# Reordered fillings, copies and weight splits in the attention stage of a one-core decoder trunk, with each round's next scores ahead of its values on TensorE

## The reference

```python
DILATED_BRANCHES = ((128, 1), (512, 4), (2048, 16))      # window, dilation

def dilated_branch(q, k, v, window, dilation):           # per head, blocks and their predecessors
    s = jnp.einsum('bhrnqd,bhrnkd->bhrnqk', qb, kk) * (Dh ** -0.5)
    s = jnp.where(mask, s, NEG)
    m = jnp.max(s, axis=-1)
    p = jnp.exp(s - m[..., None])
    l = jnp.sum(p, axis=-1)
    o = jnp.einsum('bhrnqk,bhrnkd->bhrnqd', p, vv) / l[..., None]

def dilated_attention(q, k, v):                          # the branches joined by their own maxima and sums
    wts = ls * jnp.exp(ms - jnp.max(ms, axis=0))
    return einsum(wts, os_) / sum(wts)

def mixer_ab(h, ...):
    z = h @ w_in          # queries, keys, values of both kinds of heads, and a rank-16 gate input
    ...
    return concatenate([oa, ob]) @ w_out
```

## Time and profile before

| | |
|---|---|
| median of 3 runs | 2091.09 us (2089.84 to 2091.24) |
| the profiled execution | 2089.45 us, of which the span of its instructions is 2087.6 us |
| PE busy | 2062.1 us (99%) |
| PEld, DVE, ACT, POOL busy | 81%, 70%, 44%, 42% |
| granted TensorE clock, mean | 0.998 |
| attention's steps in the trace | 223.5 us (first scores) to some 445 us |

### The profile page before, as it was taken

One profiled execution on the slowest core, in us unless ns is written; L12 is line 12 of the kernel. 1 busy time (PEld: TensorE's weight loads), 2 busy tenths in 40 slices (PEclk: granted clock), 3 DMA queues, 4 the chain that ended last, 5 costly groups with the idle time before them and its releaser, 6 DMA issues.

```text
span 2087.6 us, 26260 instructions
## 1 busy us (share of the span) xinstructions
PE 2062.1 (99%) x10166; PEld 1699.6 (81%) x10166; DVE 1467.3 (70%) x1728; ACT 916.9 (44%) x1274; POOL 873.3 (42%) x455
## 2 busy tenths in 40 slices
PE   8999999999999999999999999999999999999997
PEld 6888788878888888888888888888888888888886
DVE  6669775655976676677989504538877667677988
ACT  4231566744544444444435330225544444444444
POOL 3332112232787777760002332444877776820000
PEclk9999999999999999999999999999999999999999
DMA  4111001032222221228983111113321221249872
GB/s 169 41 31 41 21 31 32 31 122 91 81 91 91 91 81 71 91 72 306 389 298 114 51 51 31 51 41 121 111 89 63 91 91 68 84 140 384 302 282 81
DMA packets 95165, 235.95 MB, mean 113 GB/s; under 512 B 10113, under 2 KB 12482, under 8 KB 95042
## 3 DMA queue, kind: packets, MB, share of 16 engines
q1 hardware_dynamic: 93170, 229.54, 30.8%
q10 hardware_dynamic: 1872, 4.74, 0.6%
HBM read 198.59 MB, written 35.65 MB: 112 GB/s over the span
## 4 chain that ended last, share of the span: by engine, by line
PE 93%; DVE 3%; DMA 1%; SPq 1%; issue 1%; ACT 1%; POOL 0%; DVEq 0%; ACTq 0%
PE ps L1419 13%; PE ps L1420 13%; PE ps L1421 13%; PE ps L926 6%; PE ps L929 6%; PE ps L932 6%; PE ps L1453 6%; PE ps L1455 6%; PE ps L1456 6%; PE ps L1133 2%; PE ps L1135 2%; PE ps L1134 2%; PE ps L1524 1%; PE ps L1525 1%; PE ps L1526 1%; PE ps L1282 1%
## 5 line engine op out<-in xcount | busy, mean ns | idle before, releaser
L630 POOL TENSOR_TENSOR w_hi<-w_raw,ones 128x1024 fp32r<-128x1024 f32 x53 | 105.2, 1986 | 694.3 <-PE ps L932 230.2
L1419 PE MATMUL ps<-t_hi,w_hi 128*128 128x512 f32 x672 | 263.7, 392 | 0.3
L1420 PE MATMUL ps<-t_lo,w_hi 128*128 128x512 f32 x672 | 261.8, 390 | 0.0
L1421 PE MATMUL ps<-t_hi,w_lo 128*128 128x512 f32 x672 | 261.6, 389 | 0.0
L1453 PE MATMUL ps<-d_hi 128*128 128x512 f32 (+1 forms) x632 | 242.4, 384 | 0.2 <-DVE d_lo L2226 0.2
L1456 PE MATMUL ps<-d_hi,d_lo 128*128 128x512 f32 (+1 forms) x632 | 241.6, 382 | 0.0
L1455 PE MATMUL ps<-d_lo,d_hi 128*128 128x512 f32 (+1 forms) x632 | 241.6, 382 | 0.0
L690 POOL TENSOR_TENSOR w_lo<-w_sum,w_hi 128x1024 fp32r<-128x1024 f32 x84 | 231.9, 2771 | 23.2 <-ACT w_hi L2758 23.2
L690 POOL TENSOR_TENSOR w_lo<-w_raw,w_hi 128x1024 fp32r<-128x1024 f32 x84 | 157.5, 1875 | 171.0 <-ACT w_hi L2758 157.2
L1419 PE MATMUL ps<-act_hi,w_hi 128*128 128x512 f32 x504 | 196.1, 389 | 0.0
L1420 PE MATMUL ps<-act_lo,w_hi 128*128 128x512 f32 x504 | 196.1, 389 | 0.0
(11 more groups left out here) (348 smaller groups left out, 4540.4 us busy)
## 6 DMA issues: line engine op xcount, KB each, us to landing
w_raw<-w_up SPq DMA_DIRECT2D x44, 1024.0 KB, 4.8
d_ring<-w_dn SPq DMA_DIRECT2D x146, 256.0 KB, 7.9
d_ring<-g_kept SPq DMA_DIRECT2D x124, 256.0 KB, 9.6
g_kept<-gst SPq DMA_DIRECT2D x44, 512.0 KB, 2.6
w_raw<-w_in SPq DMA_DIRECT2D x24, 512.0 KB, 3.5
chain_a<-g_kept SPq DMA_DIRECT2D x44, 256.0 KB, 9.3
x_kept<-x SPq DMA_DIRECT2D x16, 512.0 KB, 9.2
x<-x_kept SPq DMA_DIRECT2D x16, 512.0 KB, 10.2
```

The costliest lines, as they stand in the source:

```text
L1419: pe.matmul(out, wh, bh, start=(fresh and j == 0), stop=False, skip_group_check=True)
L1420: pe.matmul(out, wh, bl, start=False, stop=False, skip_group_check=True)
L1421: ins = pe.matmul(out, wl, bh, start=False, stop=(j == 3), skip_group_check=True)
```

## The change

1. `low_rank` of the first four tiles of x goes behind the third tile of `first_key` (k = 2) and no longer behind the first.
2. In pair 0, GpSimd no longer waits for the end of the rope stages before it splits N_A + 4, and VectorE no longer waits for that split. VectorE's order of `out_step` and `take_part` in steps 0 to 4 changes.
3. `fills_of` leaves two pieces behind the second transposes and no longer one (but not in a pair's last round), and takes the first group from what is left.
4. `v_transposes` go ahead of the step's transposes (steps 0 to 5), in pair 0 a step later, and ScalarE's copies of them ahead of `take`.
5. In each round TensorE does the next round's scores ahead of this round's values.
6. ScalarE does `take_outs` behind the exponentials and no longer ahead.
7. In the last pair step 24 fills first and then does scores 25; `spread` goes behind `take`, in steps 1 to 3. The high part of N_WO + 3 waits for the scores of pair 2, and only the low part for `values(27)`.

```diff
@@ GpSimd @@
             low_part((N_A + 3) % 2, (N_A + 3) % 2, N_A + 5)
-            pool.wait_ge(A.rope, 20)
             low_part((N_A + 4) % 2, (N_A + 4) % 2, N_A + 6)
...
             plain(N_WO + 2, 2, (A.vn, 5 * (NHP - 1) + 3), (WO.lo, 2))
-            plain(N_WO + 3, 3, (A.pv, STEPS_A - 4))
+            n = N_WO + 3
+            pool.wait_ge(s_wdma[n % 2], 16 * (n // 2 + 1))
+            pool.wait_ge(A.s, 2 * DOUBLE)
+            pool.tensor_tensor(w_hi[:, 3, :], w_raw[:, n % 2, :], ones[:, 0:1].to_broadcast([P, 1024]), ALU.mult
+                               ).then_inc(s_whi, 1)
+            pool.wait_ge(A.pv, STEPS_A - 4)
+            low_part(n % 2, 3, n + 2)
@@ lists @@
             both = fill_of(g) + fill_of(g + 1)
-            last = len(both) - (g % SA < SA - 2)
+            last = len(both) - 2 * (g % SA < SA - 2)
             first = last - len(both) // 4
...
-            return {3: ((0, 2),), 4: ((0, 3),)}.get(s, ())
+            return {4: ((0, 2),), 5: ((0, 3),)}.get(s, ())
@@ TensorE @@
-                if k == 0 or k == 4:
+                if k == 2 or k == 4:
                     low_rank(k // 4)
...
                 for i in range(2):
                     for target, j in fills[i]:
                         piece(target, j)
+                    moves = v_moves_of(g + i)
+                    if s < SA - 2:
+                        for target, m in moves:
+                            v_transposes(target, m)
+                        moves = ()
                     transposes(g + i, 0)
                     transposes(g + i, 1)
-                    moves = v_moves_of(g + i)
...
                 for target, j in fills[2]:
                     piece(target, j)
-                for i in range(2):
-                    values(g + i)
                 scores(g + 2)
                 if g + 2 < DOUBLE:
                     scores(g + 3)
+                for i in range(2):
+                    values(g + i)
             for g in range(DOUBLE, STEPS_A):
                 hp, s = divmod(g, SA)
+                if g == DOUBLE:
+                    fill(g)
                 if g + 1 < STEPS_A:
                     scores(g + 1)
-                fill(g)
+                if g > DOUBLE:
+                    fill(g)
@@ VectorE @@
                     if s == 0:
                         take_part(0, Q1, (1, 2))
-                        dve.wait_ge(s_wsplit, N_A + 5)
-                        out_step(1, 0, 0)
-                        out_step(1, 0, 1)
+                        for step_n in range(2):
+                            out_step(1, 0, step_n)
...
                     elif s == 2:
                         take_part(1, K0, (1, 2))
-                        for step_n in range(2):
+                        take_part(1, Q0, (0,))
+                        out_step(1, 1, 0)
+                    elif s == 3:
+                        for step_n in range(1, 3):
                             out_step(1, 1, step_n)
-                    elif s == 3:
-                        take_part(1, Q0, (0,))
-                        for step_n in range(2, 5):
+                        dve.wait_ge(B.o[1], 8)
+                        take_part(1, Q0, (1, 2))
+                    elif s == 4:
+                        for step_n in range(3, 5):
                             out_step(1, 1, step_n)
-                    elif s == 4:
-                        take_part(1, Q0, (1, 2))
@@ ScalarE @@
                 if g:
-                    take_outs(g - 2)
                     if s == 0:
                         statistics_exp(hp - 1)
                     exps(g)
                     exps(g + 1)
+                    take_outs(g - 2)
                 if hp and s in (2, 4):
                     spread(hp - 1, s - 1)
+                moves_taken(g)
                 take(g, 0)
                 take(g, 1)
-                moves_taken(g)
...
+                if s == 4:
+                    moves_taken(g + 1)
                 take(g + 1, 0)
                 take(g + 1, 1)
-                moves_taken(g + 1)
+                if s != 4:
+                    moves_taken(g + 1)
...
             for g in range(DOUBLE, STEPS_A):
                 hp, s = divmod(g, SA)
                 if s == 0:
-                    take_outs(g - 2)
                     statistics_exp(hp - 1)
                     exps(g)
-                if 1 <= s < 5:
-                    spread(hp - 1, s - 1)
+                    take_outs(g - 2)
+                if s == 1:
+                    spread(hp - 1, 0)
...
                 if hp == NHP - 1:
+                    if 1 <= s < 4:
+                        spread(hp - 1, s)
                     for kk in WO_HIGHS[s]:
```

More of the change, by code:

```diff
@@ L478, in build @@
         STEPS_A = SA * NHP
+        DOUBLE = SA * (NHP - 1)
         R_A = 6 * NBP
@@ L835, in score_stat @@
             return a_class[:, hp % 2, s - NEAR, i:i + 1]
-        DOUBLE = SA * (NHP - 1)
         def scores_bank(g, h):
```

## The result

| | before | after |
|---|---|---|
| median of 10 runs each | 2091.3 us (2089.5 to 2093.5) | 2096.8 us (2095.0 to 2100.5) |
| profiled execution, and its span | 2089.45, 2087.6 us | 2098.7, 2096.9 us |
| PE busy | 2062.1 us | 2068.0 us |
| mean granted TensorE clock | 0.998 | 0.995 |

The ratio of after to before is 1.0026 (95%: 1.0018 to 1.0035): 5.5 us slower. The predicted time, 2094.7 us, is 2.1 us low. The result lies in the range and in the forecast's own one, but just over the bound of 0.2%, so that "slower" holds, to which I had given 0.29, and not "within 0.2%", to which I had given 0.55. The interval reaches down to 0.18%, so it is a narrow call. The two profiled executions lie further apart than the medians, 9.3 us: before's is near the fast end of its kernel's times, and after's the second slowest of its ten.

A forecast was written before the change was run, and what follows sets the result against it. TensorE, busy 99% of the span, bounds the kernel. Terms −0.2 + 0.3 − 1.0 + 1.7 + 2.8 = +3.6 us take the median from 2091.09 to 2094.7 us; the 8 in 10 range is 2085.0 to 2098.5.

The forecast's parts named there:

- the forecast's own one: The main forecast's own range, 2092.5 to 2097 us, with a chance of 0.48.
- the bound of 0.2%: What a measurement of this kernel can tell from no change: about 0.2%, 4.2 us.
- start: Moved product of four x tiles: the third tile ends 0.2 us sooner, −0.2; bounds −1.7 and +1.7.
- pair 0: Two stalls of 1.2 and 1.6 us merge into two others; V0 starts about when it did: +0.3.
- rounds of pairs 1 and 2, with g = 22: Both waits for a_vc go, −1.0; `take_outs` ahead of `take` costs 0.4 us at g = 22.
- turn to the last pair: Scores 25's wait goes, −1.6, but TensorE idles 2.7 us for V0: +1.7 with g = 22's 0.4.
- end of the steps, from g = 25: GpSimd's high and low part each fall ahead of one `attention_low`; TensorE ends the steps 2.8 us later: +2.8.
- behind the attention: TensorE's work after the attention: nothing moves, as no stall that VectorE or GpSimd sets is within reach.
- Sharing by bandwidth: VectorE and GpSimd share the SBUF port pair by bandwidth: collisions cost 2.5 not 4.3 us, the end about +1.
- the stalls go and nothing takes their place: Rival, chance 0.16: the attention's seven stalls are covered, V0 taken within 1.6 us of scores 25: 2084.1 us.
- the end doesn't collide: Rival, chance 0.17: at the end of the steps +2.8 becomes about 0, the sum +0.8: 2091.9 us.
- `take` stalls 12 times: Rival, chance 0.14: `take_outs` ahead of `take` stalls second transposes in most of 12 rounds, 3.6 us more: 2098.3 us.

The follow-up runs named there:

- e2_split_back: Changed kernel, but the high part of N_WO + 3 waits for values(27) again, as before: 2092.7 us, ratio 1.0011.
- e3_start_back: Changed kernel, but low_rank of the first four x tiles is behind the first tile of first_key again: 2095.5 us, ratio 1.0024.
- e9_pause_long: Kernel before with four added TensorE pauses of 3.0 to 3.1 us idle in the projections for pairs 2 and 3: 2110.3 us, ratio 1.0090.
- e11_split_only: Kernel before with only the high part of N_WO + 3 put behind the last paired exponentials, its low part still behind values(27): 2091.6 us, ratio 1.0007.
- e6_best: Changed kernel with V0 ahead of tops(25), N_WO + 3's split and the start as before, and another new pair 0 order: 2084.6 us, ratio 0.9966.
- e1_v0_first: Changed kernel, but at the turn to the last pair VectorE takes V0 ahead of tops(25): 2093.2 us, ratio 1.0009.
- e7_swap_only: Kernel before with edit 5 alone, the next round's scores ahead of this round's values: 2089.2 us, ratio 0.9990.
- e8_pause_short: Kernel before with four added TensorE pauses of 1.2 us idle in the projections for pairs 2 and 3: 2095.3 us, ratio 1.0024.
- the last kernel: e6_best, but the split of N_WO + 3 waits for the output projection's first results instead of values(27): 2083.3 us, ratio 0.9967.

## Why the prediction was right in its places and low in its size

Each term against the shift of after's profile, with the stretches at half clock apart. One of 3.41 us is put at 1.6, as above. For the turn, `e2_split_back` and `e3_start_back` have V0's wait of 2.9 us without a stretch and lose 1.8 us each from g = 23 to g = 25; after loses 4.7 there, so its stretch of 6.83 us is put at 2.9:

| term | forecast | measured without the stretches | stretches |
|---|---|---|---|
| start | −0.2 | +0.9 (the later rise of the clock within it) | |
| pair 0 | +0.3 | +0.1 | +1.6 |
| rounds of pairs 1 and 2, with g = 22 | −0.6 | −1.2 | |
| turn to the last pair | +1.3 | +1.8 | +2.9 |
| end of the steps, from g = 25 | +2.8 | +2.4, wait and stretch together | |
| behind the attention | 0 | +0.8 | |
| sum | +3.6 | +4.8 | +4.5 |

The last row before the sum looks like chance and not like the change: a wait for d_lo of 0.9 us or more, where before has 0.2, stands near that place in seven of the fourteen profiles, `e9_pause_long` and `e11_split_only` among them, and is missing in `e2_split_back`, `e3_start_back` and `e6_best`.

**The turn** held in every part: scores 25 without a wait, and V0's transposes idle 2.9 us where 2.7 were forecast, for the reason given; taking V0 first (`e1_v0_first`) removed it. The rival by which the stalls go and nothing takes their place fell here, at the point that it named: V0 was taken 4.6 us behind scores 25 and not 1.6.

**The end** held as well. L1956 in front took 1.95 us for 1.33, the forecast's 0.6. The pair at 6.2 us is 3.9 later than alone, where the forecast had 1.9 + 2.4 = 4.3, whole instruction by whole instruction. Sharing by bandwidth, at 2.5 us in all, doesn't fit: neither the size nor that each `attention_low` ends 1.1 us behind the end of a GpSimd instruction. As the Trainium skill has it ("SBUF — State Buffer", section "Who interferes with whom"), VectorE with two inputs in SBUF and GpSimd hold one port pair in turn, and 6.21, 6.25, 4.04 and 2.35 us for the same pair beside two, two, one and no split in its way agree. The rival "the end doesn't collide" is out by after's own trace, and `e2_split_back` and `e11_split_only` show that the split order makes the collision. What I had as one wait for `wo_piece` and `values(28)` together, 3 to 4 us, came as 2.1 us and two pieces at half pace. In `e1_v0_first`, where no stretch stood ahead to hide it, `values(28)` waited 1.4 us behind `wo_piece`'s 2.2, which makes 3.6.

**Pair 0** came out at nothing without its stretch, as forecast, by two stalls that moved: a_sh at 2.1 us, and the other one at the exponentials of step 4. With the stretch of 1.6 us that four of the five profiles with this order have it is a loss, which the forecast didn't have.

**The rounds** gained 1.2 us: both waits for a_vc are gone, and the 0.4 us that I charged to g = 22 left no wait in the trace. The rival by which `take` stalls 12 times fell with it.

**The start** was outside its term and inside its bounds. The clock rose at 17.28 us in after and at 15.54 in before, but over all the profiles it rose at 15.2 to 17.3 us with the new order (three) and at 13.6 to 16.5 with the old (eleven). The product of the second four x tiles comes 0.5 us later in the mean of the three than in that of the eleven. The order's own effect is smaller than that scatter, and `e3_start_back` couldn't tell it from nothing.

**The step that failed** is one sentence that I applied to the start alone: that the trace of before doesn't show what the clock does when a pause stands in another place. I let every stall cost its own length. The trace of before has three pauses of 1.2 to 1.6 us in the attention and no stretch behind any of them, and this I took for the rule. The change turned them into pauses of 1.4, 2.1, 2.9 and 2.1 us. Over the fourteen profiles, counting each pause of TensorE by the idle time that the profile gives it, between the clock's rise at the start and the end: 25 from 0.9 to 1.3 us had no half-level stretch behind them; of 19 from 1.35 to 1.65 us, six had one (three of these six came 4 us behind another pause); of 12 from 1.9 to 2.2, seven; of 7 from 2.9 to 3.2, four. Four more stretches, all at 1182 to 1210 us, had no such pause ahead of them, but all four began within 1.4 us of the end of the thirteen matmuls of 1x1. It is a chance for each, not a rule, and it also scatters the times: of after's ten executions five had a mean granted clock of 0.997 (median 2095.5 us) and five of 0.994 or 0.995 (2098.0 us), while of 77 of the kernel before 48 had 0.998 (2090.1 us) and 25 had 0.997 (2092.6 us). Taken at the same mean clock of 0.997, after is 2.9 us slower (2095.5 against 2092.6), near the forecast's 3.6, and the other 2.6 us of the measured 5.5 would be the clock's. The mean clock is known to three places only, each worth 2.1 us, so this division is rough; and it groups the executions by a clock that the change itself lowers. That a pause can cause a stretch is shown by the pauses put in. What decides which of two equal ones does is open.

## What to carry to other kernels

When an edit makes scores or pieces come sooner, look at what the engine that must empty their bank has ahead of that copy in its own list: V0's wait of 2.9 us was the longest in the attention, and taking V0 ahead of `tops(25)` cures it. On a kernel that TensorE bounds, price a pause as long as those here at its length and a chance of another 1.6 us, and one long pause dearer than the same idle time in short pieces (four of 1.2 us had no stretch behind them, four of 3.1 us had three): so two small stalls that an edit makes a little longer and brings close together, as in pair 0 here, are no even trade. And put long GpSimd work with both operands in SBUF where VectorE works from PSUM, or, as in the last kernel, where TensorE doesn't wait for it yet; ahead of a VectorE instruction with two SBUF inputs it costs up to the split's whole length. Last, look in the trace where a moved instruction really went: the last edit helped by doing the opposite of what was meant.

## What was not expected of the hardware

- The half-level stretches last 3.41 us each or twice that (6.83), wherever they were found, and the clock then returns at once to 1.00 with TensorE as busy as ahead of the pause.
- The same 1.6 us pause for a_sh at the same place in the same instructions had a stretch behind it in two profiles (`e7_swap_only`, `e8_pause_short`) and none in four.
